# Chunk stage of a hybrid layer: even heads on the lower, odd heads on the upper half of the partitions

## The reference

```python
s = s * w[:, :, None, :] + sa[..., None] * (kk * a)[:, :, None, :] + v[..., None] * k[:, :, None, :]   # sa = s @ -kk
y = einsum('bhvk,bhk->bhv', s, r)
```

## Time and profile before

| | |
|---|---|
| runs | 4111.47, 4121.16, 4129.18 us; median 4121.16 |
| the profiled execution | 4116.76 us; span of its core 4114.9 us |
| granted TensorE clock, whole span | 0.962 |
| busy, whole span | TensorE 92%, VectorE 56%, ScalarE 47%, GpSimd 15% |
| the chunk stage's loop | from about 1230 to 2220 us of the span |

### The profile page before, as it was taken

One profiled execution on the slowest core, in us unless ns is written; L12 is line 12 of the kernel. 1 busy time (PEld: TensorE's weight loads), 2 busy tenths in 40 slices (PEclk: granted clock), 3 DMA queues, 4 the chain that ended last, 5 costly groups with the idle time before them and its releaser, 6 DMA issues. The chain is left out here.

```text
span 4114.9 us, 93756 instructions
## 1 busy us (share of the span) xinstructions
PE 3772.4 (92%) x39634; PEld 3168.5 (77%) x39634; DVE 2290.6 (56%) x3788; ACT 1947.2 (47%) x3029; POOL 613.5 (15%) x601
## 2 busy tenths in 40 slices
PE   7999999999979899989898978997599999999993
PEld 6778878888868788888887767786488888888883
DVE  5533524434337777777776975455554545454445
ACT  5533434434336666666665443243144444444443
POOL 1000000000012122212210333200011111111111
PEclk9999999999989999999998989998699999999997
DMA  7566565555542222222323466654366666666667
GB/s 277 189 180 190 179 194 152 159 155 157 151 119 76 80 76 66 80 80 62 105 64 90 117 222 215 197 181 160 148 210 215 211 213 213 212 217 209 219 209 296
DMA packets 334966, 673.42 MB, mean 164 GB/s; under 512 B 32828, under 2 KB 213156, under 8 KB 316936
## 3 DMA queue, kind: packets, MB, share of 16 engines
q1 hardware_dynamic: 307592, 580.68, 43.3%
q0 software_dynamic: 27008, 87.46, 7.4%
HBM read 524.89 MB, written 143.15 MB: 162 GB/s over the span
## 5 line engine op out<-in xcount | busy, mean ns | idle before, releaser
L112 PE MATMUL fro__acc<-fro__hT_hi,fro__wh 128*128 128x512 f32 (+1 forms) x1608 | 626.0, 389 | 11.8 <-DVE fro__hT_lo L2671 8.9
L113 PE MATMUL fro__acc<-fro__hT_hi,fro__wl 128*128 128x512 f32 (+1 forms) x1608 | 614.3, 382 | 0.0
L114 PE MATMUL fro__acc<-fro__hT_lo,fro__wh 128*128 128x512 f32 (+1 forms) x1608 | 614.1, 382 | 0.0
L2677 DVE TENSOR_TENSOR fro__wl<-prj__w,fro__wh 128x1024 fp32r<-128x1024 f32 x201 | 246.2, 1225 | 640.6 <-ACT fro__wh L2460 640.6
L2088 DVE TENSOR_TENSOR fin__wl<-fin__raw,fin__wh 128x4096 fp32r<-128x4096 f32 x96 | 424.6, 4423 | 318.4 <-ACT fin__wh L2032 318.4
L2032 ACT ACTIVATE fin__wh<-fin__raw 128x4096 fp32r<-128x4096 f32 x96 | 348.4, 3629 | 190.4 <-PE exp__acc L114 190.3
L112 PE MATMUL exp__acc<-fin__wh,exp__xh 128*128 128x512 f32 x1024 | 400.9, 391 | 0.7 <-DVE exp__xl L2093 0.7
L113 PE MATMUL exp__acc<-fin__wh,exp__xl 128*128 128x512 f32 x1024 | 399.3, 390 | 0.0
L114 PE MATMUL exp__acc<-fin__wl,exp__xh 128*128 128x512 f32 x1024 | 399.2, 390 | 0.0
L112 PEld LDWEIGHTS fro__acc<-fro__hT_hi,fro__wh 128*128 128x128 f32 x1608 | 304.7, 189 | 77.9 <-issue 22.2
L113 PEld LDWEIGHTS fro__acc<-fro__hT_hi,fro__wl 128*128 128x128 f32 x1608 | 304.8, 190 | 59.2 <-issue 3.6
(11 more groups left out here) (460 smaller groups left out, 8121.9 us busy)
## 6 DMA issues: line engine op xcount, KB each, us to landing
fin__raw<-in_w_x SPq DMA_DIRECT2D x96, 2048.0 KB
prj__w<-in_w_z SPq DMA_DIRECT2D x201, 512.0 KB, 4.2
s_zT<-fro__pool SPq DMA_DIRECT2D x128, 256.0 KB, 4.7
fro__wm<-in_w_mod POOLq DMA_DIRECT2D x16, 1024.0 KB, 5.6
mix__gate<-s_zT SPq DMA_DIRECT2D x64, 256.0 KB, 4.3
prj__xin<-in_tokens SPq DMA_DIRECT2D x18, 512.0 KB, 5.4
rwc__kS<-s_kS SPq DMA_DIRECT2D x36, 256.0 KB, 3.1
rwc__kkn<-s_kkn SPq DMA_DIRECT2D x36, 256.0 KB, 3.3
```

Of the source, the lines that this page charges most:

```text
L112: pe.matmul(out, sh, mh, start=first, stop=False)
L113: pe.matmul(out, sl, mh, start=False, stop=False)
L114: return pe.matmul(out, sh, ml, start=False, stop=last)
L2677: ve.tensor_tensor(wl[s % 3][:, :, :], w[s % 3][:, :, :], wh[s % 3][:, :, :], ALU.subtract).then_inc(split_lo, 1)
```

## The change

The chunk stage's rows change places. Afterwards heads 0, 2, 4, 6 lie on partitions 0 to 63 and heads 1, 3, 5, 7 on 64 to 127; the two chunks lie along the row. `PB[t]` holds the right side in columns 0 to 255 and the outputs in 256 to 511. `BK[:, 2q + s]` is head pair q of chunk s. R, U and yo become 128x256. `Hb` loses its zeros. Each TensorE burst of the turns alternates between the two diagonal quarters of the array (partitions 0-63 to 0-63, 64-127 to 64-127). `turn` is made of 64x64 float32 products with the identity in place of the transposes. `solve` adds onto the right side that stands in PSUM: for that the last refinement adds TT32 - I (`TTm`, a new tile, made by a new GpSimd operation) in place of TT32. The rows of y are stored in two DMAs a turn, each with runs of 64 channels, in place of one with runs of 512. The diff, cut to its changed lines and the functions that they stand in:

```diff
@@ -177,9 +177,10 @@
...
-        R, U, yo = [[sb(f"{n}{t}", [P, HALF]) for t in range(2)] for n in ("R", "U", "yo")]
+        R, U, yo = [[sb(f"{n}{t}", [P, 4 * WD]) for t in range(2)] for n in ("R", "U", "yo")]
+        TTm = sb("TTm", [P, NG, GH, HC])
...
-        Hb = [sb(f"Hb{d}", [P, 4, 2, WD]) for d in range(2)]
+        Hb = [sb(f"Hb{d}", [P, 4, WD]) for d in range(2)]
@@ -192,6 +193,7 @@
...
+        part = lambda k, q: slice(256 * k + WD * q, 256 * k + WD * q + WD)
@@ -202,7 +204,7 @@
...
-                 rhc0=1, rhc1=1, uc0=1, uc1=1, yc0=1, yc1=1, al=1, rho=1, bonp=1, imt=2, tth=1)
+                 rhc0=1, rhc1=1, uc0=1, uc1=1, yc0=1, yc1=1, al=1, rho=1, bonp=1, imt=2, tth=1, tti=1)
@@ -247,7 +249,9 @@
             def store_rows(j, t):
...
-                sp.dma_start(T["y"][j % 2, ds(slab_at(j) + HC * s, HC), :], yo[t][side(1 - s), :]).then_inc(y_out[t], 16)
+                heads = T["y"][j % 2, ds(slab_at(j) + HC * s, HC), :].rearrange("t (q e c) -> t e q c", q=4, e=2)
+                for e in range(2):
+                    sp.dma_start(heads[:, e, :, :], yo[t][side(e), :].rearrange("t (q c) -> t q c", q=4)).then_inc(y_out[t], 16)
@@ -285,7 +289,7 @@
...
-                sp.wait_ge(y_out[t], 16 * SLABS + START)
+                sp.wait_ge(y_out[t], 32 * SLABS + START)
@@ -299,7 +303,7 @@
...
-                gp.memset(Hb[d][:, :, :, :], 0.0)
+                gp.memset(Hb[d][:, :, :], 0.0)
@@ -332,6 +336,8 @@
...
                 gp.tensor_copy(TTh[:, :, :, :], TT32[:, :, :, :]).then_inc(S["tth"], 1)
+                gp.tensor_tensor(TTm[:, :, :, :].rearrange("p g h c -> p (g h) c"), TT32[:, :, :, :].rearrange("p g h c -> p (g h) c"),
+                                 ident2[:, None, :].to_broadcast([P, NG * GH, HC]), ALU.subtract).then_inc(S["tti"], 1)
@@ -421,21 +427,18 @@
...
             def right_side(j, t):
-                z = side(turn_of(j, t))
...
-                cp(R[t][z, :], PB[t][z, :], f"rhc{t}")
+                cp(R[t][:, :], PB[t][:, 0:256], f"rhc{t}")
...
             def solved(j, t):
-                z = side(turn_of(j, t))
...
-                cp(U[t][z, :], PB[t][z, :], f"uc{t}")
+                cp(U[t][:, :], PB[t][:, 0:256], f"uc{t}")
...
             def outputs(j, t):
-                z = side(1 - turn_of(j, t))
...
-                    act.wait_ge(y_out[t], 16 * j + START)
-                cp(yo[t][z, :], PB[t][z, :], f"yc{t}")
+                    act.wait_ge(y_out[t], 32 * j + START)
+                cp(yo[t][:, :], PB[t][:, 256:512], f"yc{t}")
...
             def inverses(j):
@@ -604,23 +607,18 @@
...
             def refine(r, j, g):
...
-                tt(Gr[j % 2][:, g, :, :], h4(RB[g]), TT32[:, g, :, :], ALU.add).then_inc(S["gd"], 1)
+                if r == 2:
+                    ve.wait_ge(S["tti"], at("tti", j))
+                tt(Gr[j % 2][:, g, :, :], h4(RB[g]), (TTm if r == 2 else TT32)[:, g, :, :], ALU.add).then_inc(S["gd"], 1)
...
             def state(j, t):
...
-                hb = Hb[d][:, :, :, :]
-                for o in range(2):
-                    r = side(o)
-                    ins = tt(H[d][r, :, :], EB[r, 0:256].rearrange("p (q c) -> p q c", q=4), hb[r, :, o, :], ALU.add)
-                ins.then_inc(S[f"hadd{t}"], 1)
+                tt(H[d][:, :, :], EB[:, 0:256].rearrange("p (q c) -> p q c", q=4), Hb[d][:, :, :], ALU.add).then_inc(S[f"hadd{t}"], 1)
...
-                for o in range(2):
-                    r = side(o)
-                    ins = tt(Hb[d][r, :, o, :], H[d][r, :, :], F[u % B][r, k, :, :], ALU.mult)
-                ins.then_inc(S[f"hup{t}"], 1)
+                tt(Hb[d][:, :, :], H[d][:, :, :], F[u % B][:, k, :, :], ALU.mult).then_inc(S[f"hup{t}"], 1)
@@ -717,10 +715,10 @@
...
-                        for o in range(2):
-                            for s in range(2):
-                                r, c = side(o), (256 * (q % 2) + 128 * k)
-                                m = mm(MB[z][o][side(s), c:c + 128].rearrange("p (a c) -> p a c", a=2), src[r, q, side(s)],
+                        for s in range(2):
+                            for r in map(side, range(2)):
+                                c = 256 * (q % 2) + 128 * k
+                                m = mm(MB[z][s][r, c:c + 128].rearrange("p (a c) -> p a c", a=2), src[r, q, side(s)],
...
                 m.then_inc(S["m1"], 1)
@@ -732,8 +730,10 @@
...
-                for q in range(4):
-                    m = pe.transpose(f4(dst)[:, q, :], src[:, q, :], ident[:, :])
+                for s in range(2):
+                    for q in range(4):
+                        for r in map(side, range(2)):
+                            m = mm(dst[r, part(s, q)], src[r, q, side(s)], ident2[r, :], start=True, stop=True)
                 m.then_inc(S["trm"], 1)
...
             def bonus(j):
@@ -806,61 +806,60 @@
                 m.then_inc(S["gm"], 1)
...
             def values(j, t):
-                u, z, o = j % B, side(turn_of(j, t)), side(1 - turn_of(j, t))
+                u, s = j % B, turn_of(j, t)
...
-                for n in range(WH):
-                    c = slice(WD * n, WD * n + WD)
-                    mm(PB[t][z, c], BK[u][z, n, 2, :], v_t[u][z, c], start=(n == 0), stop=False, skip_group_check=True)
-                    mm(PB[t][o, c], BK[u][z, n, 3, :], v_t[u][z, c], start=(n == 0), stop=False, skip_group_check=True)
+                for q in range(4):
+                    for k in range(2):
+                        for r in map(side, range(2)):
+                            mm(PB[t][r, part(k, q)], BK[u][r, 2 * q + s, 2 + k, :], v_t[u][r, part(s, q)], start=(q == 0 and k == 0), stop=False,
+                               skip_group_check=True)
...
             def from_state(j, t):
...
-                z, o = side(s), side(1 - s)
...
-                    c = slice(P * q, P * q + P)
-                    hb = Hb[j % 2][:, q, :, :].rearrange("p o c -> p (o c)")
-                    m = mm(PB[t][z, c], AR[u][:, q, 0, z], hb, start=False, stop=True, skip_group_check=True)
-                    m = mm(PB[t][o, c], AR[u][:, q, 1, z], hb, start=False, stop=False, skip_group_check=True)
+                    for k in range(2):
+                        for r in map(side, range(2)):
+                            m = mm(PB[t][r, part(k, q)], AR[u][r, q, k, side(s)], Hb[j % 2][r, q, :], start=False, stop=False, skip_group_check=True)
                 m.then_inc(S[f"rhm{t}"], 1)
...
             def solve(j, t):
-                z = side(turn_of(j, t))
+                s = turn_of(j, t)
...
-                for n in range(WH):
-                    c = slice(WD * n, WD * n + WD)
-                    m = mm(PB[t][z, c], Gr[j % 2][z, n // GH, n % GH, :], R[t][z, c], start=True, stop=True)
+                for q in range(4):
+                    n = 2 * q + s
+                    for r in map(side, range(2)):
+                        m = mm(PB[t][r, part(0, q)], Gr[j % 2][r, n // GH, n % GH, :], R[t][r, part(0, q)], start=False, stop=True, skip_group_check=True)
                 m.then_inc(S[f"uum{t}"], 1)
...
             def state(j, t):
-                u, z = j % B, side(turn_of(j, t))
+                u, s = j % B, turn_of(j, t)
...
-                for key, val in ((kappa_t[u], v_t[u]), (beta_t[u], U[t])):
-                    for n in range(WH):
-                        c = slice(WD * n, WD * n + WD)
-                        m = mm(EB[side(n % 2), WD * (n // 2):WD * (n // 2) + WD], key[z, c], val[z, c],
-                               start=(val is not U[t] and n < 2), stop=val is U[t], skip_group_check=True)
+                for key, val, k in ((kappa_t[u], v_t[u], s), (beta_t[u], U[t], 0)):
+                    for q in range(4):
+                        for r in map(side, range(2)):
+                            m = mm(EB[r, part(0, q)], key[r, part(s, q)], val[r, part(k, q)],
+                                   start=(val is not U[t] and q == 0), stop=val is U[t], skip_group_check=True)
                 m.then_inc(S[f"sm{t}"], 1)
...
             def outputs(j, t):
...
-                z, o = side(s), side(1 - s)
...
-                for n in range(WH):
-                    c = slice(WD * n, WD * n + WD)
-                    m = mm(PB[t][o, c], BK[u][z, n, 1, :], U[t][z, c], start=False, stop=True, skip_group_check=True)
+                for q in range(4):
+                    for r in map(side, range(2)):
+                        m = mm(PB[t][r, part(1, q)], BK[u][r, 2 * q + s, 1, :], U[t][r, part(0, q)], start=False, stop=True, skip_group_check=True)
                 m.then_inc(S[f"ym{t}"], 1)
...
```

## The result

The changed kernel takes 4127.48 us in the median of 20 runs, the kernel before, on the same chip, 4119.18. The ratio is 1.0023, 95% interval 1.0012 to 1.0033: 0.2% slower, within the 0.5% that the prediction counted as no change. The forecast was 4074 us, in a range of 4042 to 4112.

A forecast was written before the change was run, and what follows sets the result against it. TensorE's fixed list of bursts was taken as the bound for most of the loop, with ScalarE's copies before couple 4. Minus 1.2 and minus 0.1 us a slab, times 36, gave 47 us: 4074 us, range 4042 to 4112.

The forecast's parts named there:

- rival B: Turns not covered: second mask stays late, the inverse's seed waits for v_t in full; slab gains 0.3 us, 4110; chance 0.14.
- Part 2: TensorE's `values`, `state` and `pairs` bursts: equal numbers of products at the pace they have now, so no change.
- Part 1: `solve` and `outputs`, twice each per slab: diagonal pairs take bursts from 1.13 to 0.70 us, minus 0.43 to 0.46 each.
- Part 4: `turn`, three times a slab: transposes become 32 instructions of float32 products, 0.99 us each, plus 1.37 us a slab.
- Part 3: `from_state`, twice a slab: 16 instructions in 1.02 us become 32 in 0.99; minus 0.05 us each.
- Part 5: ScalarE's six copies R, U, yo: 0.59 us each, then 381 ns as 128x256; minus 0.21 us each.
- the path: From `from_state` through ScalarE's copies to couple 4 minus 1.2 us, `double` of level 4 to seed minus 0.1, per slab.
- rival A: ScalarE isn't the limit before couple 4, which no longer waits for Tb; 2.0 us a slab, 4049 by the median; chance 0.14.
- Part 6 and 7: VectorE's state update: minus 0.9 us before the second mask, minus 1.5 at the other; GpSimd's TTm: plus 1.4 us, hidden.
- Part 8: Stores of y: two issues become four, with runs of 256 B; taken to cost nothing.
- rival D: Stores of y land in twice 6.4 us and ScalarE waits 4 us for yo; 97 us slower, 4218; chance 0.04.
- C: Turns: diagonal quarters don't run together with fresh float32 loads and one PSUM bank; plus 1.6 us a slab, 4179; chance 0.06.

The follow-up runs named there:

- after_whole_store: The changed kernel with y of a turn stored by one DMA of 128 runs of 1 KB, rows in another order; 4118.10 us, ratio 1.0010 to the kernel before.

## Why the prediction was wrong

The measured time lies above the whole range, and the gain that was forecast did not come. That the kernel ended so near the old time is a balance of three terms (the other parts' gain, the pairs' loss and the waits for instructions), not the "within" that rival B stood for. The period tells it, as an estimate that takes every wait for instructions as on the path. Without the waits for instructions a slab takes 27.75 - 0.7 = 27.0 us before and 28.06 - 1.7 = 26.4 after: the change brings 0.6 to 0.7 us a slab, 24 us, and the waits take 1.0, 35 us, back.

1. **Part 2, "`values`, `state`, `pairs`: equal numbers at the pace they have now", is the step that failed.** For `values` and `state` it holds: their products stream 64 columns, use two quarters in turn before and after, and take 0.031 in either arrangement. For the pairs I had no row at all. They stream 128 columns, and before the change they went round all four quarters at 0.029 us a step; on the two diagonal quarters that the new layout has, they take 0.056. The row that would have shown it stands beside `outputs` in the same timeline, and `from_state` gave the scale: two halves of the array in turn, 128 columns, 0.107 us for two. What the runs show in place of "nothing": a burst of 32 takes 1.78 us in place of 0.94, and the run that takes 0.83 off each of a slab's two bursts is 1.1 us a slab faster, some 40 us.
2. **Waits for instructions were missing from the sum.** The prediction said of TensorE's idle time that "two of those waits matter", both for ScalarE. 18.5 us in 700 were put to issue already, and a change with 15% more instructions made them 43.0, 1.0 us a slab more. Half goes with the burst of loads; why the rest stays is open.
3. **Part 1**, `solve` and `outputs` at 0.70: right. **Part 4**, turns at 0.99: measured 0.93, right. **Part 3** was too small: `values` and `from_state` together go from 1706.94 - 1704.84 = 2.10 to 1715.67 - 1713.76 = 1.91, minus 0.19 where 0.05 was forecast.
4. **Part 5 and the path.** The copies are 0.38 to 0.40 as priced, but ScalarE holds couple 4 back far less than forecast: its wait is 5.9 us in 700 after, 18 times, where 0.9 a slab (some 22 us) was forecast. Without the waits for instructions, couple 0 to couple 4 shrinks by 12.65 - 10.31 = 2.3 us, more than the 1.9 of rival A. Some of that may be what the other engines caught up while TensorE waited; the whole balance, 27.0 - 26.4 and the 1.1 of the pairs on top, says about 1.7 a slab for the parts that were forecast at 1.3. Rival A gives this part's size better than the forecast, though its sign, couple 4 without a wait, did not come: the 18 waits are about as many as the 16 before.
5. **Part 6 and 7.** VectorE's update is 0.42 and 0.42 to 1.25 (the product beside GpSimd), the seed waits no more, and TTm is hidden: right.
6. **Part 8**, the stores: nothing, right. Two of 64 KB in place of one of 128 KB, they land sooner than before, where rival D had doubled the time (changed kernel, the stores at L254; before in the earlier trace rows):

```profile
DMA to landing us min/median/max: 2.0/2.9/4.0
```

The rule of the Trainium skill (DMA: Bandwidth & Descriptors, Specifications) that runs under 512 B are read, modified and written may hold, but here it neither lengthens the landing nor the kernel.

Rivals B, C and D did not happen. C had the right place in mind, diagonal quarters, with the wrong products: the turns keep 0.029. The Trainium skill (TensorEngine Tiling (Array Packing), Gotcha 1: PSUM Pressure) would have row tiles kept off one bank; the run with two banks shows that for diagonal quarters the bank makes no difference to the pace: 0.056 us a step with one and with two.

## What to carry to other kernels

When a layout changes which quarters of the array small products use, read the step of every burst that moves, in number of quarters and in columns streamed, also of those whose count stays: here products of 64 columns kept 0.031 us a step on whichever two quarters took turns, and those of 128 lost half their pace from four quarters to two. Count TensorE's instructions, and look at its idle time put to issue before taking a dense list as free; if waits fall 127 products apart, the program is late, and loads issued in one burst are worth spreading over the stage. Here that last edit, found on the way, is worth three times what the whole change moved.

## What the runs showed of the hardware

- Float32 products of 64 rows and 64 columns of weights, streaming 128 columns: 0.029 us a step over four quarters of the array, 0.056 over two diagonal ones, whether they write one PSUM bank or two. Streaming 64 columns: 0.030 over two, 0.061 in one.
- TensorE's program comes in packets of 16.4 KB, about 256 instructions, never less than 3.2 us apart. A late one stops the engine in the middle of a burst, for up to 3.1 us in the changed kernel and 4.7 in after_whole_store, and the engine goes on 1.2 to 1.6 us after it has landed. Six loads of 256 KB issued back to back make 18.5 - 2.2 = 16 us of such waits in 700 in the kernel before; spread over a slab of 27 us, they make next to none there.
- One late packet can be followed by others: in the slab shown, waits of 1.36, 0.89 and 0.88 us come 4.5 and 4.0 us apart, each one packet after the last.
